# Gated linear attention scores computed on 64x64 diagonal squares, with the rotation split by token half, in a two-layer hybrid decoder trunk on one core

## The chip, the core and the metric

The kernel runs on one core of one Trainium2 chip. The metric is the device time of one execution in microseconds (us). The engines are PE (matrix multiply, with PEld for its weight loads), DVE (vector), ACT (scalar), POOL (GpSimd) and SP (which only issues transfers here). Each works through its own list of instructions in order; they meet at semaphores.

## What is computed

Two layers, 256 tokens, 1024 features. In each, one projection feeds three mixers (retention, RWKV-7, gated linear attention), whose outputs go through an output projection; then comes a retrieval over 16384 one-neuron experts. The change lies in the first two of these parts:

```python
z = h @ w_in[l]
z_ret, z_rwkv, z_gla = _split(z, GROUP_SIZES)
# retention: q and k are rotated, 4 heads of 64
q, k = _rotary(q, pos), _rotary(k, pos) * (RET_DK ** -0.5)
scores = jnp.einsum('bhid,bhjd->bhij', qc, kc) * dmat
# gated linear attention: 4 heads, keys of 48 (padded to 64 in the kernel), values of 96
bcum = jnp.cumsum(gc, axis=-2)
diff = bcum[..., :, None, :] - bcum[..., None, :, :]
dec = jnp.where(mask, jnp.exp(jnp.where(mask, diff, 0.0)), 0.0)
attn = jnp.sum(qc[..., :, None, :] * kc[..., None, :, :] * dec, axis=-1)
o = o_inter + jnp.einsum('bhij,bhjv->bhiv', attn, vc)
```

The kernel computes the gated scores of all 256 tokens as one lower triangle, by levels. Level 0 is the diagonal. Level n (1 to 8) holds the pairs whose tokens lie in the two halves of one block of 2^n tokens: both sides are scaled by the exponential of their distance to the block's middle, multiplied, and only the square of that level is kept.

## The kernel before, in words

The input projection is cut into 15 groups of 256 output columns. For a group, SP loads 1 MB of weights into one of two ring slots, ACT copies them in four parts to a rounded form (`w_high`, L1009), DVE forms the remainder of each part (`w_lows`, L1408), and PE multiplies with three products for each part (L417 to L419 for groups 0 to 7, L433 to L435 from group 8 on). The rounded form and the remainder have one buffer for each part: ACT may start part m of group g+1 when PE is done with part m of group g. ACT then moves the group's sum out of PSUM (`evac_group`, L1038 or L1040). Groups 10 to 13 are split by token half (`group(10, 0)`, `group(10, 1)`), each half with 24 matmuls of 128x256; a group in one piece has 48.

Between the half groups stand the levels. For level n, POOL forms the two differences (`level_gates(n)`, L1999 and L2000), ACT takes the exponential (L1220), POOL multiplies with queries and keys (`level_operand(n)`, L2008 and L2009), PE computes the scores (`level(n)`, L722), and DVE copies them under the level's mask into the sum `GACC` (L1656). For levels 0 to 7 PE runs, for each of two token tiles of 128 and four heads, one matmul with 64 rows (the key features), 128 columns of weights and 128 moving columns; heads with even and odd number use the two row halves of the array. PE's part of level n waits for `gx_ready` (POOL) and, where the scores go to the PSUM banks 4 and 5 or 6 and 7 in turn, for the readers of these banks. POOL's `level_operand(n)` waits until PE is done with level n-2, since its two buffers are used in turn.

Beside that, DVE rotates queries and keys of the retention (`rotate`, L1628 to L1633: six operations for each token tile), PE turns them (`turn_qk`, L682), ACT copies them out (L1228), PE multiplies them (`scores`, L690 and L691), DVE applies the decay (L1642 and L1643), and PE forms the outputs (`retention_outputs`, L702 to L705). All orders are written out by hand, one list for each engine, at the end of the engine's block. Behind group 14 follows the RWKV part (`units`, L517, L530 and L549), on 64x64 tiles of the array for part of its matmuls.

Of the kernel before, what the change touches and what calls it, by code (L numbers as in the profile page):

```python
# [33 lines left out]
U32 = mybir.dt.uint32  # L34
F16 = mybir.dt.float16
I32 = mybir.dt.int32
ALU = mybir.AluOpType
# [3 lines left out]
P = 128  # L41
S = 256
NT = S // P
# [57 lines left out]
def trunk(nc, x_in, w_in, w_out, cols, small, rows, norm_final, w_q, keys, u_t, v_t, const, xconst, out):  # L101
    with ExitStack() as ctx:
# [73 lines left out]
        LOWB, UPB, EYEB = LOWS[:, :, 0, :], LOWS[:, 0, 1, :], LOWS[:, 1, 1, :]  # L176
# [17 lines left out]
        GACC = BIG[:, decays:decays + 1536].rearrange("p (t h n) -> p t h n", t=3, h=GH)  # L194

# [67 lines left out]
        gacc_zero = sem("gacc_zero")  # L263
# [129 lines left out]
        def _(pe):  # L393
# [111 lines left out]
            def units():  # L505

                pe.wait_ge(ab_ready, 1)
                pe.wait_ge(gs_out, 9)

# [198 lines left out]
            def level(n, bank):  # L708
# [3 lines left out]
                for t in range(NT if n < 8 else 1):  # L712
                    for h in range(GH):
                        r, b = slice(64 * (h % 2), 64 * (h % 2) + 64), h // 2
                        if n == 0:
                            lhs, rhs = GQK[r, 2 + b, t * P:(t + 1) * P], GQK[r, b, t * P:(t + 1) * P]
                        elif n < 8:
                            lhs = rhs = GX[r, n % 2, b, t * P:(t + 1) * P]
                        else:
                            lhs, rhs = GX[r, n % 2, b, 0:P], GX[r, n % 2, b, P:S]  # L720
                        o = PS[:, bank + h % 2, (2 * t + b) * P:(2 * t + b + 1) * P]
                        mm = pe.matmul(o, lhs, rhs, start=True, stop=True)  # L722
                mm.then_inc(gs_done, 1)

            def gla_outputs():

                pe.wait_ge(proj_out, N_IN)
                for t in range(NT):
# [152 lines left out]
            with pe.Fori(0, L) as l:  # L881
# [23 lines left out]
                turn_qk()  # L905
                group(10, 1)
                pe.wait_ge(gs_out, 2)
                level(2, 4)
                pe.wait_ge(rot_out, 2)
                scores(0, 6)  # L910
                group(11, 0)
                pe.wait_ge(score_out, 2)
                level(3, 6)
                group(11, 1)
                pe.wait_ge(gs_out, 3)
                scores(1, 4)
                pe.wait_ge(gs_out, 4)
                level(4, 6)
                group(12, 0)
                pe.wait_ge(score_out, 4)  # L920
                level(5, 4)
                pe.wait_ge(gs_out, 5)
                retention_outputs()
                group(12, 1)
                pe.wait_ge(gs_out, 6)
                level(6, 4)
                group(13, 0)
                pe.wait_ge(ret_o_out, 1)
                level(7, 6)
                group(13, 1)  # L930
                pe.wait_ge(gs_out, 7)
                level(8, 4)
                group(14)
# [33 lines left out]
        def _(act):  # L967
# [52 lines left out]
            def w_split_in(g):  # L1020

                w_split(g)
# [128 lines left out]
            with act.Fori(0, L) as l:  # L1151
# [74 lines left out]
                for t in range(NT):  # L1226
                    act.wait_ge(rot_done, t + 1)
                    act.copy(QKT[:, :, t * P:(t + 1) * P], PS[:, 6 + t, :].rearrange("p (b n) -> p b n", b=4)).then_inc(rot_out, 1)  # L1228
                level_exp(3)
                w_split_in(11)  # L1230
                evac_group(10)
                level_exp(4)
                level_exp(5)
# [3 lines left out]
                act.copy(TI[:, :, :], EYEB.unsqueeze(1).broadcast_to([P, 12, 64])).then_inc(eye_ready, 1)  # L1237
                w_split_in(12)
                evac_group(11)
                level_exp(6)  # L1240
                act.copy(TB[:, :, :], EYEB.unsqueeze(1).broadcast_to([P, 12, 64])).then_inc(eye_ready, 1)
# [6 lines left out]
                level_exp(8)  # L1248
                w_split_in(14)
# [125 lines left out]
        def _(dve):  # L1375
# [244 lines left out]
            def rotate():  # L1620

                dve.wait_ge(proj_out, 10)
                for t in range(NT):
                    z = ZRET[:, t, 0:512].rearrange("p (g h c) -> p g h c", g=8, h=2)
                    rope = XC[:, X_ROPE + 64 * t:X_ROPE + 64 * (t + 1)].rearrange("p (a c) -> p a c", a=2)
                    cos, sin = (rope[:, a, :].unsqueeze(1).broadcast_to([P, 8, 32]) for a in range(2))
# [540 lines left out]
```

## Time and profile before

| | us |
|---|---|
| median of 3 runs (2082.27 to 2087.98) | 2083.05 |
| the profiled execution | 2079.46 |
| its span in the trace | 2077.7 |
| PE busy in the span | 2019.5 |
| stretch of the levels, layer 1 of 2 (81.60 to 131.70) | 50.10 |
| stretch of the levels, layer 2 of 2 (1111.90 to 1161.00) | 49.10 |

The profile shows one execution. A row of the timeline has its start in us from the span's start, its length in us, the engine, the line, the operation, what it writes and reads, the shape and the count; in brackets stands the idle time of the engine before it and who ended it. A matmul's modelled end reaches over the start of the next one, so that what a piece of work costs PE is read from start to start. An fp32 matmul appears as two records, so x16 is eight instructions. For the loop over the two layers the trace has the same lines twice.

### The profile page before, as it was taken

The page shows a single profiled execution, that of the slowest core. Times are in us where ns is not written, and L with a number is a line of the kernel's source. Part 1 is how long each engine was busy: PE and PEld are TensorE (multiplying, and loading weights), DVE is VectorE, ACT ScalarE, POOL GpSimd, SP SyncE. Part 2 cuts the span into 40 slices and gives each one's busy share as a digit, 9 for nine tenths or more (in the row PEclk, how much of TensorE's full clock was granted, in tenths as well). Part 3 has the DMA queues.
Part 4 walks back from the last instruction along what each step waited for, and adds up shares of the span by engine and source line. Part 5 has one row for each costly group of instructions (what it writes and reads, how often), then busy time and mean ns, then how long its engine had stood idle before and what let it go on. Part 6 is the DMA issues. An engine that isn't in the chain of part 4 may idle for free.

```text
span 2077.7 us, 47159 instructions
## 1 busy us (share of the span) xinstructions
PE 2019.5 (97%) x15444; PEld 1836.8 (88%) x15444; DVE 1416.5 (68%) x3068; ACT 1332.2 (64%) x3144; POOL 394.2 (19%) x348
## 2 busy tenths in 40 slices
PE   8999999999999999999999999999999999999996
PEld 8896899999999888888798959999999998888885
DVE  6863579588887666666668534985888876666665
ACT  6640555899999555555565315669999985555554
POOL 0312056522222000000004200764222220000000
PEclk9999999999999999999999999999999999999998
DMA  6311544444444555555553125444444445555554
GB/s 240 123 63 57 176 155 162 162 162 162 162 162 163 190 193 194 189 199 186 182 197 122 43 82 183 145 172 168 162 162 162 162 162 184 201 184 200 186 197 173
DMA packets 47471, 338.95 MB, mean 163 GB/s; under 512 B 5648, under 2 KB 5776, under 8 KB 6928
## 3 DMA queue, kind: packets, MB, share of 16 engines
q1 hardware_dynamic: 47376, 337.73, 45.5%
q8 instruction: 54, 0.88, 0.2%
q14 instruction: 41, 0.34, 0.0%
HBM read 336.66 MB, written 1.05 MB: 163 GB/s over the span
## 4 chain that ended last, share of the span: by engine, by line
PE 88%; DVE 7%; ACT 2%; DMA 1%; issue 1%; SPq 0%; DVEq 0%; ACTq 0%; PEldq 0%
PE ps L859 11%; PE ps L860 11%; PE ps L861 11%; PE ps L829 10%; PE ps L831 10%; PE ps L830 10%; PE ps L417 3%; PE ps L418 3%; PE ps L419 3%; PE ps L751 2%; PE ps L839 1%; PE ps L840 1%; PE ps L433 1%; DVE expert_lo L1786 1%; PE ps L435 1%; PE ps L434 1%
## 5 line engine op out<-in xcount | busy, mean ns | idle before, releaser
L829 PE MATMUL ps<-h_t_hi,expert_hi 128*128 128x256 f32 x2048 | 591.3, 289 | 12.3 <-DVE expert_lo L1786 8.6
L830 PE MATMUL ps<-h_t_lo,expert_hi 128*128 128x256 f32 x2048 | 578.5, 282 | 0.0
L831 PE MATMUL ps<-h_t_hi,expert_lo 128*128 128x256 f32 x2048 | 578.2, 282 | 0.0
L1980 POOL TENSOR_TENSOR expert_lo<-w_ring,expert_hi 128x512 fp32r<-128x512 f32 x204 | 289.7, 1428 | 719.2 <-ACT expert_hi L1050 717.6
L829 PEld LDWEIGHTS ps<-h_t_hi,expert_hi 128*128 128x128 f32 x2048 | 391.6, 191 | 15.6 <-ACT big L1055 8.3
L859 PE MATMUL ps<-expert_hi,act_hi 128*128 128x512 f32 x1008 | 392.1, 389 | 0.0
L860 PE MATMUL ps<-expert_lo,act_hi 128*128 128x512 f32 x1008 | 392.1, 389 | 0.0
L861 PE MATMUL ps<-expert_hi,act_lo 128*128 128x512 f32 x1008 | 392.1, 389 | 0.0
L830 PEld LDWEIGHTS ps<-h_t_lo,expert_hi 128*128 128x128 f32 x2048 | 391.9, 191 | 0.0
L831 PEld LDWEIGHTS ps<-h_t_hi,expert_lo 128*128 128x128 f32 x2048 | 391.6, 191 | 0.0
L1050 ACT CAST expert_hi<-w_ring 128x512 fp32r<-128x512 f32 x512 | 308.4, 614 | 98.2 <-PE ps L831 85.1
L1790 DVE TENSOR_TENSOR expert_lo<-w_ring,expert_hi 128x512 fp32r<-128x512 f32 x512 | 331.0, 687 | 6.7 <-ACT expert_hi L1130 6.0
L1140 ACT CAST act_hi<-big 128x256 fp32r (+1 forms) x256 | 103.9, 406 | 318.2 <-PE ps L861 318.2
L1130 ACT CAST expert_hi<-w_ring 128x512 fp32r<-128x512 f32 x512 | 291.9, 617 | 3.3 <-PE ps L831 3.2
L1786 DVE TENSOR_TENSOR expert_lo<-w_ring,expert_hi 128x512 fp32r<-128x512 f32 x308 | 217.7, 719 | 107.2 <-ACT expert_hi L1050 104.2
L1794 DVE TENSOR_TENSOR act_lo<-big,act_hi 128x256 fp32r<-128x256 f32 x256 | 108.8, 425 | 260.6 <-ACT act_hi L1140 260.6
L861 PEld LDWEIGHTS ps<-expert_hi,act_lo 128*128 128x128 f32 x1008 | 189.2, 188 | 39.4
L859 PEld LDWEIGHTS ps<-expert_hi,act_hi 128*128 128x128 f32 x1008 | 189.2, 188 | 39.2
L860 PEld LDWEIGHTS ps<-expert_lo,act_hi 128*128 128x128 f32 x1008 | 189.2, 188 | 39.1
L1408 DVE TENSOR_TENSOR expert_lo<-w_ring,expert_hi 128x512 fp32r<-128x512 f32 x188 | 131.7, 726 | 72.2 <-ACT expert_hi L1009 70.1
L1009 ACT CAST expert_hi<-w_ring 128x512 fp32r<-128x512 f32 x176 | 106.4, 619 | 107.8 <-PE ps L419 63.0
L417 PE MATMUL ps<-h_t_hi,expert_hi 128*128 128x256 f32 x512 | 146.4, 286 | 2.1 <-DVE expert_lo L1408 1.6
(310 smaller groups left out, 3133.8 us busy)
## 6 DMA issues: line engine op xcount, KB each, us to landing
w_ring<-u_t SPq DMA_DIRECT2D x128, 1024.0 KB, 4.8
w_ring<-v_t SPq DMA_DIRECT2D x128, 1024.0 KB, 4.8
w_ring<-w_in SPq DMA_DIRECT2D x32, 1024.0 KB, 4.9
w_ring<-w_q SPq DMA_DIRECT2D x16, 1024.0 KB, 4.8
w_ring<-w_out SPq DMA_DIRECT2D x8, 1024.0 KB, 4.8
big<-xconst SPq DMA_DIRECT2D x2, 1666.0 KB, 9.3
big<-keys SPq DMA_DIRECT2D x2, 1024.0 KB, 4.7
big<-rows SPq DMA_DIRECT2D x2, 576.0 KB, 11.2
```

The lines of the kernel that those rows point to most:

```text
L417: pe.matmul(o, w_hi_m[:, c, :], HTH[:, d, :], start=d == 0, stop=False)
L829: pe.matmul(o, w_hi[:, c, :], HTH[:, d, :], start=d == 0, stop=False)
L830: pe.matmul(o, w_hi[:, c, :], HTL[:, d, :], start=False, stop=False)
L831: mm = pe.matmul(o, w_lo[:, c, :], HTH[:, d, :], start=False, stop=d == DC - 1)
L859: pe.matmul(o, a_hi_t, EH[:, m % 4, :], start=start, stop=False, skip_group_check=True)
L860: pe.matmul(o, a_hi_t, EL[:, m % 4, :], start=False, stop=False, skip_group_check=True)
L861: mm = pe.matmul(o, a_lo_t, EH[:, m % 4, :], start=False, stop=True, skip_group_check=True)
L1050: act.copy(EH[:, m % 4, :], RING[:, m // 4, (m % 4) * 512:(m % 4 + 1) * 512]).then_inc(u_hi, 1)
L1130: act.copy(EH[:, m % 4, :], RING[:, m // 4, (m % 4) * 512:(m % 4 + 1) * 512]).then_inc(v_hi, 1)
L1786: dve.tensor_tensor(EL[:, m % 4, :], RING[:, m // 4, (m % 4) * 512:(m % 4 + 1) * 512], EH[:, m % 4, :].bitcast(F32), ALU.subtract).then_in ...
L1790: dve.tensor_tensor(EL[:, m % 4, :], RING[:, m // 4, (m % 4) * 512:(m % 4 + 1) * 512], EH[:, m % 4, :].bitcast(F32), ALU.subtract).then_in ...
L1980: pool.tensor_tensor(EL[:, m % 4, :], RING[:, m // 4, (m % 4) * 512:(m % 4 + 1) * 512], EH[:, m % 4, :].bitcast(F32), ALU.subtract).then_i ...
```

## The change

Levels 0 to 6 only ever need the two 64x64 squares on the diagonal of a 128-token tile. Now PE computes those alone: 16 matmuls with 64 rows, 64 columns of weights and 64 moving columns in the place of 8 with 128 and 128. Level 7 computes only the square of first-half keys and second-half queries. DVE copies levels 0 to 6 under folded masks (`UPF`, which POOL adds up from the left and right half of each mask) into a compact sum `GAC` of half the width, and level 7 straight into its place in `GACC`. ACT fills the zero square of `GACC` and copies the compact sum into its two diagonal squares behind level 6. Level 8 is as it was. All levels now use banks 4 and 5, and the retention banks 6 and 7. The orders on PE, ACT and DVE are written anew: the rotation is done by token half at two places, `turn_qk` comes behind group 11, which is in one piece, and group 14 is in two halves. The diff, cut to its core:

```diff
@@ -173,7 +173,9 @@
         LOWS = XC[:, X_LOW:X_LOW + 768].rearrange("p (n a b) -> p n a b", n=6, a=2)
-        LOWB, UPB, EYEB = LOWS[:, :, 0, :], LOWS[:, 0, 1, :], LOWS[:, 1, 1, :]
+        UPS = XC[:, X_UP:X_UP + 768].rearrange("p (n a b) -> p n a b", n=6, a=2)
+        LOWB, UPF, EYEB = LOWS[:, :, 0, :], UPS[:, :, 0, :], LOWS[:, 1, 1, :]
+        UPB = UPF[:, 0]
         VTOK = KKN.rearrange("p c n -> p (c n)").rearrange("p (k n) -> p k n", k=NT)
@@ -192,6 +194,8 @@
+
+        GAC = BIG[:, decays + 1728:decays + 2240].rearrange("p (t h n) -> p t h n", t=NT, h=GH)
@@ -506,6 +510,7 @@
                 pe.wait_ge(gs_out, 9)
+                pe.wait_ge(ret_o_out, 1)
 
@@ -712,19 +717,23 @@
-                        if n == 0:
-                            lhs, rhs = GQK[r, 2 + b, t * P:(t + 1) * P], GQK[r, b, t * P:(t + 1) * P]
-                        elif n < 8:
-                            lhs = rhs = GX[r, n % 2, b, t * P:(t + 1) * P]
+                        at = (2 * t + b) * 64
+                        if n < 7:
+                            for i in range(2):
+                                s = slice(t * P + 64 * i, t * P + 64 * i + 64)
+                                lhs, rhs = (GQK[r, 2 + b, s], GQK[r, b, s]) if n == 0 else (GX[r, n % 2, b, s], GX[r, n % 2, b, s])
+                                mm = pe.matmul(PS[64 * i:64 * i + 64, bank + h % 2, at:at + 64], lhs, rhs, start=True, stop=True)
+                        elif n == 7:
+                            mm = pe.matmul(PS[0:64, bank + h % 2, at:at + 64], GX[r, n % 2, b, t * P:t * P + 64], GX[r, n % 2, b, t * P + 64:(t + 1) * P],
+                                           start=True, stop=True)
...
-                            lhs, rhs = GX[r, n % 2, b, 0:P], GX[r, n % 2, b, P:S]
-                        o = PS[:, bank + h % 2, (2 * t + b) * P:(2 * t + b + 1) * P]
-                        mm = pe.matmul(o, lhs, rhs, start=True, stop=True)
+                            mm = pe.matmul(PS[:, bank + h % 2, b * P:(b + 1) * P], GX[r, n % 2, b, 0:P], GX[r, n % 2, b, P:S], start=True, stop=True)
...
+                pe.wait_ge(gacc_full, 3)
@@ -902,35 +911,35 @@
-                turn_qk()
...
+                group(11)
+                turn_qk()
+                pe.wait_ge(gs_out, 3)
+                level(3, 4)
...
-                group(11, 0)
+                group(12, 0)
+                pe.wait_ge(gs_out, 4)
+                level(4, 4)
...
-                level(3, 6)
-                group(11, 1)
-                pe.wait_ge(gs_out, 3)
-                scores(1, 4)
-                pe.wait_ge(gs_out, 4)
-                level(4, 6)
-                group(12, 0)
+                scores(1, 6)
+                group(12, 1)
+                pe.wait_ge(gs_out, 5)
+                level(5, 4)
...
-                level(5, 4)
-                pe.wait_ge(gs_out, 5)
...
-                group(12, 1)
+                group(13, 0)
...
-                group(13, 0)
-                pe.wait_ge(ret_o_out, 1)
-                level(7, 6)
...
+                level(7, 4)
+                group(14, 0)
+                pe.wait_ge(gs_out, 8)
...
-                group(14)
+                group(14, 1)
@@ -1223,22 +1232,23 @@
-                for t in range(NT):
-                    act.wait_ge(rot_done, t + 1)
-                    act.copy(QKT[:, :, t * P:(t + 1) * P], PS[:, 6 + t, :].rearrange("p (b n) -> p b n", b=4)).then_inc(rot_out, 1)
-                level_exp(3)
...
-                level_exp(4)
-                level_exp(5)
+                level_exp(3)
...
+                act.activation(GACC[64:128, 0:2, :, 0:64], EYEB[64:128].unsqueeze(1).unsqueeze(1).broadcast_to([64, NT, GH, 64]), ACT.Identity, scale=0.0).then_inc(gacc_full, 1)
...
+                for t in range(NT):
+                    act.wait_ge(rot_done, t + 1)
+                    act.copy(QKT[:, :, t * P:(t + 1) * P], PS[:, 6 + t, :].rearrange("p (b n) -> p b n", b=4)).then_inc(rot_out, 1)
...
+                level_exp(4)
+                level_exp(5)
+                act.copy(TB[:, :, :], EYEB.unsqueeze(1).broadcast_to([P, 12, 64])).then_inc(eye_ready, 1)
...
-                act.copy(TB[:, :, :], EYEB.unsqueeze(1).broadcast_to([P, 12, 64])).then_inc(eye_ready, 1)
@@ -1246,6 +1256,9 @@
+                act.wait_ge(gs_out, 7)
+                act.copy(GACC[0:64, 0:2, :, 0:64], GAC[0:64]).then_inc(gacc_full, 1)
+                act.copy(GACC[64:128, 0:2, :, 64:128], GAC[64:128]).then_inc(gacc_full, 1)
@@ -1617,21 +1630,20 @@
-            def rotate():
+            def rotate(t):

                 dve.wait_ge(proj_out, 10)
-                for t in range(NT):
-                    z = ZRET[:, t, 0:512].rearrange("p (g h c) -> p g h c", g=8, h=2)
...
+                z = ZRET[:, t, 0:512].rearrange("p (g h c) -> p g h c", g=8, h=2)
...
@@ -1643,7 +1655,8 @@
-            masks = [ident] + [XC[:, X_UP + P * n:X_UP + P * (n + 1)] for n in range(7)]
+            gac = GAC.rearrange("p t (c r) n -> p t r c n", r=2)
+            masks = [EYEB] + [UPF[:, n] for n in range(6)]
@@ -1651,9 +1664,11 @@
-                    if n < 8:
-                        mask = masks[n].bitcast(U32).unsqueeze(1).unsqueeze(1).broadcast_to([P, NT, 2, P])
-                        ins = dve.copy_predicated(gacc[:, 0:2, r], mask, PS[:, bank + r, :].rearrange("p (t c n) -> p t c n", t=NT, c=2))
+                    if n < 7:
+                        mask = masks[n].bitcast(U32).unsqueeze(1).unsqueeze(1).broadcast_to([P, NT, 2, 64])
+                        ins = dve.copy_predicated(gac[:, :, r], mask, PS[:, bank + r, 0:256].rearrange("p (t c n) -> p t c n", t=NT, c=2))
+                    elif n == 7:
+                        ins = dve.tensor_copy(gacc[0:64, 0:2, r, :, 64:128], PS[0:64, bank + r, 0:256].rearrange("p (t c n) -> p t c n", t=NT, c=2))
@@ -1889,22 +1904,24 @@
+                dve.wait_ge(folded, 1)
...
-                rotate()
+                rotate(0)
...
+                rotate(1)
...
+                w_lows(12)
+                level(3, 4)
...
-                level(3, 6)
-                w_lows(12)
-                decayed(1, 4)
-                level(4, 6)
+                level(4, 4)
+                decayed(1, 6)
+                w_lows(13)
...
-                w_lows(13)
...
-                level(7, 6)
...
+                level(7, 4)
@@ -2024,14 +2041,14 @@
-                pool.tensor_tensor(UPB, XC[:, X_UP:X_UP + 64], XC[:, X_UP + 64:X_UP + 128], ALU.add)
+                pool.tensor_tensor(UPF, UPF, UPS[:, :, 1, :], ALU.add)
...
-                pool.memset(GACC[:, 0:2, :, :], 0.0).then_inc(gacc_zero, 1)
+                pool.memset(GAC[:, :, :, :], 0.0).then_inc(gacc_zero, 1)
```

How the lists of two engines read around the rotation. On PE, from group 10 to the scores of the first two retention heads, before (L722 is a level, L433 to L435 a group, L682 `turn_qk`, L690 and L691 `scores`):

```order
L722 MATMUL ps<-big 128x128 [waits gx_ready,gs_out]
L722 MATMUL ps<-big 128x128 x7
L682 MATMUL ps<-const_sb,big 128x128 [waits rot_ready,gg_out]
L682 MATMUL ps<-const_sb,big 128x128 x3
L682 MATMUL ps<-const_sb,big 128x128 [waits rot_ready]
L682 MATMUL ps<-const_sb,big 128x128 x3
...
L722 MATMUL ps<-big 128x128 [waits gx_ready,gs_out]
L722 MATMUL ps<-big 128x128 x7
L690 MATMUL ps<-big 128x256 [waits rot_out]
```

And now (L725 is a level, L687 `turn_qk`, L695 `scores`; at the two marks stand the second half of group 10 and the whole of group 11):

```order
L725 MATMUL ps<-big 64x64 [waits gx_ready,gs_out]
L725 MATMUL ps<-big 64x64 x15
...
L725 MATMUL ps<-big 64x64 [waits gx_ready,gs_out]
L725 MATMUL ps<-big 64x64 x15
...
L687 MATMUL ps<-const_sb,big 128x128 [waits rot_ready,gg_out]
L687 MATMUL ps<-const_sb,big 128x128 x3
L687 MATMUL ps<-const_sb,big 128x128 [waits rot_ready]
L687 MATMUL ps<-const_sb,big 128x128 x3
L725 MATMUL ps<-big 64x64 [waits gx_ready,gs_out]
L725 MATMUL ps<-big 64x64 x15
L695 MATMUL ps<-big 128x256 [waits rot_out]
```

The transposes moved from between levels 1 and 2 to behind group 11, with level 3 between them and the scores. On DVE, from level 0 to level 2, now (L1669 is a level, L1640 to L1645 one token half of the rotation, L1421 the four remainders of a group; before, all twelve rows of the rotation stood between levels 0 and 1):

```order
L1669 COPY_PREDICATED big<-big,ps 128x4x64 [waits gs_done,gacc_zero,folded]
L1669 COPY_PREDICATED big<-big,ps 128x4x64
L1640 TENSOR_TENSOR big<-big 128x8x32 [waits proj_out]
...
L1669 COPY_PREDICATED big<-big,ps 128x4x64 [waits dve_step,gs_out,gs_done]
L1669 COPY_PREDICATED big<-big,ps 128x4x64
L1421 TENSOR_TENSOR expert_lo<-w_ring,expert_hi 128x512 [waits w_hi] x4
L1640 TENSOR_TENSOR big<-big 128x8x32 [waits proj_out]
...
L1669 COPY_PREDICATED big<-big,ps 128x4x64 [waits dve_step,gs_out,gs_done]
```

The second half of the rotation went behind level 1 and the remainders of group 11.

## Rows read from the trace of the kernel before

**Rows 1.** The page: busy times, chain by engine, transfers of the input weights.

```profile
PE 2019.5 (97%) x15444; PEld 1836.8 (88%) x15444; DVE 1416.5 (68%) x3068; ACT 1332.2 (64%) x3144; POOL 394.2 (19%) x348
...
PE 88%; DVE 7%; ACT 2%; DMA 1%; issue 1%; SPq 0%; DVEq 0%; ACTq 0%; PEldq 0%
...
w_ring<-w_in SPq DMA_DIRECT2D x32, 1024.0 KB, 4.9
```

**Rows 2.** Busy time by stretch: from:to, length, engines, granted clock, DMA.

```profile
81.60:131.70 50.10, 46.53 (x425) 43.93 (x424) 33.19 (x57) 20.73 (x36) 19.61 (x25) 0.97 0.31 109
...
91.55:96.08 4.53, 4.53 (x27) 4.40 (x25) 3.11 (x5) 2.86 (x5) 2.80 (x4) 0.62 0.00 2
...
140.00:150.00 10.00, 10.00 (x236) 9.48 (x234) 6.83 (x16) 7.32 (x37) 0.00 (x0) 1.00 0.01 2
...
1111.90:1161.00 49.10, 45.14 (x426) 42.43 (x424) 34.04 (x57) 20.78 (x36) 20.06 (x25) 1.00 0.31 111
```

**Rows 3.** Timeline of PE, first layer, levels 0 and 1 and the transposes.

```profile
81.62 1.16 PE L722 MATMUL ps<-big 64*128 64x128 f32 x16
82.71 0.39 PE L433 MATMUL ps<-expert_hi,h_t_hi 128*128 128x256 f32 x1
...
85.78 1.16 PE L722 MATMUL ps<-big 64*128 64x128 f32 x16
88.61 0.63 PE L682 MATMUL ps<-const_sb,big 128*128 128x128 f32 x4 [1.67 <-DVEq L1634]
91.14 0.66 PE L682 MATMUL ps<-const_sb,big 128*128 128x128 f32 x4 [1.90 <-DVEq L1634]
91.55 0.36 PE L433 MATMUL ps<-expert_hi,h_t_hi 128*128 128x256 f32 x1
```

**Rows 4.** Timeline of PE, second layer: the second transposes and level 3.

```profile
1121.47 0.66 PE L682 MATMUL ps<-const_sb,big 128*128 128x128 f32 x4 [1.90 <-DVEq L1634]
...
1130.28 1.16 PE L722 MATMUL ps<-big 64*128 64x128 f32 x16 [0.39 <-DVE big L1643]
```

**Rows 5.** Timeline of PE, first layer: matmuls of the RWKV part.

```profile
135.28 0.93 PE L530 MATMUL ps<-big 64*64 64x64 f32 x48
136.14 2.10 PE L517 MATMUL ps<-big 64*128 64x256 f32 x16
138.17 0.92 PE L549 MATMUL ps<-big 64*64 64x64 f32 x24
139.01 0.49 PE L517 MATMUL ps<-big 64*128 64x256 f32 x2
```

**Rows 6.** Timeline of DVE, both layers: levels, rotation, remainders of the weights.

```profile
83.65 1.39 DVE L1656 COPY_PREDICATED big<-const_sb,ps 128x512 f32<-128x512 uint32 x2
...
85.47 0.87 DVE L1629 TENSOR_TENSOR big<-big 128x256 f32<-128x256 f32 x1
...
88.89 0.42 DVE L1629 TENSOR_TENSOR big<-big 128x256 f32<-128x256 f32 x1
...
115.46 2.79 DVE L1408 TENSOR_TENSOR expert_lo<-w_ring,expert_hi 128x512 fp32r<-128x512 f32 x4 [2.95 <-ACT expert_hi L1009]
...
126.49 0.75 DVE L1658 COPY big<-ps 128x256 f32<-128x256 f32 x2
...
1123.82 4.10 DVE L1408 TENSOR_TENSOR expert_lo<-w_ring,expert_hi 128x512 fp32r<-128x512 f32 x4 [0.88 <-ACT expert_hi L1009]
```

**Rows 7.** Timeline of ACT, first layer: a copy out of PSUM and a fill.

```profile
89.27 0.59 ACT L1228 COPY big<-ps 128x512 f32<-128x512 f32 x1 [5.91 <-PE ps L682]
...
118.57 0.85 ACT L1245 ACTIVATE big<-big 64x768 f32<-64x768 f32 x1
```

**Rows 8.** Timeline of POOL, first layer: a mask's fold, a difference, a level's product.

```profile
18.35 1.10 POOL L2026 TENSOR_TENSOR big<-big 128x384 f32<-128x384 f32 x1 [11.36 <-DMA big<-rows]
...
85.45 0.61 POOL L1999 TENSOR_TENSOR big<-big 128x256 f32<-128x256 f32 x1 [0.18 <-POOL big L2009]
...
93.78 1.18 POOL L2009 TENSOR_TENSOR big<-big 128x256 f32<-128x256 f32 x1
```

More of the change, by code:

```diff
@@ L262, in trunk @@
         gla_o, gla_o_out = sem("gla_o"), sem("gla_o_out")
-        gacc_zero = sem("gacc_zero")
+        gacc_zero, gacc_full = sem("gacc_zero"), sem("gacc_full")
         silu_ready, gcum_ready, sq_ready = sem("silu_ready"), sem("gcum_ready"), sem("sq_ready")
@@ L1618, in rwkv_out @@
                 link(dve.tensor_tensor(O, O, GBIAS, ALU.add))
-            def rotate():
+            def rotate(t):
                 dve.wait_ge(proj_out, 10)
-                for t in range(NT):
-                    z = ZRET[:, t, 0:512].rearrange("p (g h c) -> p g h c", g=8, h=2)
-                    rope = XC[:, X_ROPE + 64 * t:X_ROPE + 64 * (t + 1)].rearrange("p (a c) -> p a c", a=2)
-                    cos, sin = (rope[:, a, :].unsqueeze(1).broadcast_to([P, 8, 32]) for a in range(2))
-                    tmp = RTMP[:, t, :].rearrange("p (g c) -> p g c", g=8)
-                    dve.tensor_tensor(ROT[:, t, :, 0, :], z[:, :, 0, :], cos, ALU.mult)
-                    link(dve.tensor_tensor(tmp, z[:, :, 1, :], sin, ALU.mult))
-                    link(dve.tensor_tensor(ROT[:, t, :, 0, :], ROT[:, t, :, 0, :], tmp, ALU.subtract))
-                    dve.tensor_tensor(ROT[:, t, :, 1, :], z[:, :, 0, :], sin, ALU.mult)
-                    link(dve.tensor_tensor(tmp, z[:, :, 1, :], cos, ALU.mult))
-                    link(dve.tensor_tensor(ROT[:, t, :, 1, :], ROT[:, t, :, 1, :], tmp, ALU.add))
-                    dve.sem_inc(rot_ready, 1)
+                z = ZRET[:, t, 0:512].rearrange("p (g h c) -> p g h c", g=8, h=2)
+                rope = XC[:, X_ROPE + 64 * t:X_ROPE + 64 * (t + 1)].rearrange("p (a c) -> p a c", a=2)
+                cos, sin = (rope[:, a, :].unsqueeze(1).broadcast_to([P, 8, 32]) for a in range(2))
+                tmp = RTMP[:, t, :].rearrange("p (g c) -> p g c", g=8)
+                dve.tensor_tensor(ROT[:, t, :, 0, :], z[:, :, 0, :], cos, ALU.mult)
+                link(dve.tensor_tensor(tmp, z[:, :, 1, :], sin, ALU.mult))
+                link(dve.tensor_tensor(ROT[:, t, :, 0, :], ROT[:, t, :, 0, :], tmp, ALU.subtract))
+                dve.tensor_tensor(ROT[:, t, :, 1, :], z[:, :, 0, :], sin, ALU.mult)
+                link(dve.tensor_tensor(tmp, z[:, :, 1, :], cos, ALU.mult))
+                link(dve.tensor_tensor(ROT[:, t, :, 1, :], ROT[:, t, :, 1, :], tmp, ALU.add))
+                dve.sem_inc(rot_ready, 1)
             def decayed(b, bank):
```

## The prediction

> **What bounds the kernel now.** I read the page first: PE is busy 97% of the span and holds 88% of the chain that ended last [rows 1]. So the question is only what the stretch of the levels costs PE. Then the busy time by stretch: of the 50.10 us in layer 1 PE is busy 46.53, in layer 2 45.14 of 49.10, and no other engine comes above 34.04 [rows 2]. The timeline of PE shows where the missing 3.6 and 4.0 us lie. Level 1 starts at 85.78 and costs 1.09 from start to start, as level 0 does (81.62 to 82.71); PE is then free at 86.87, but the first four transposes start at 88.61 and the second four at 91.14, both released by DVE's rotation; each four cost 0.41 (91.14 to 91.55) [rows 3]. The wait is 91.55 - 86.87 - 2 x 0.41 = 3.86 us. Layer 2 has the same wait, its second part again 1.90 us by the profile's count, and 0.39 us more before level 3, for DVE's decay, which reads the banks that level 3 writes [rows 4]. One thing more is seen in layer 1 alone: the half group behind the transposes takes 4.53 us at a granted clock of 0.62 [rows 2], where the half group at full clock takes 85.78 - 82.71 = 3.07 [rows 3]. Some of its matmuls ran at the lower level of 1.2 GHz, after PE had stood still twice.
>
> **The change part by part.**
>
> The levels on PE. The trace has the new shape already: L530 is a run of matmuls with 64 rows, 64 weight columns and 64 moving columns that goes through all four quarters of the array, two neighbours with the same rows and different output halves, as the new loop does. It takes 24 of them (48 records) from 135.28 to 136.14, 0.86 us, so 0.036 us each [rows 5]. Sixteen give 0.57 us for 1.09: 0.52 saved, seven times a layer. Level 7 has eight such matmuls into one output half, so two quarters take turns; the run that uses two quarters is L549, 12 in 0.84 us (138.17 to 139.01), 0.070 each [rows 5]. Eight give 0.56, 0.53 saved. A layer saves 7 x 0.52 + 0.53 = 4.17, both 8.3 us. The bounds are 0.57 and, at the rate of L549, 16 x 0.070 = 1.12 us for a level, which would save nothing. I take the first, since L530 has the same quarters in the same order. As the program is PE's nearly throughout, this falls on the path if nothing else is late.
>
> A rule of the Trainium skill speaks against this part: TensorE: Matmul & The Clock Gate, in Part 3, Packing small matmuls, says that a weight load overlaps running matmuls only where the row group differs, and the new inner loop keeps the row group. By that rule every second load would stand open and a level would gain little or nothing. This case's trace doesn't agree: in L530 every second matmul keeps its rows too, and it is the cheapest run of the three [rows 5].
>
> The rotation. It is 3.6 us of DVE for the first token half (from 85.04, where level 0's copy ends, to the release at 88.61) and 2.53 for the second (88.61 to 91.14) [rows 3, 6]. Now PE has other work while it goes on. I follow both lists from 81.62, with DVE done with the remainders of group 10 at 83.65. DVE: level 0 to 84.35, first half to 87.95, level 1 to 88.65, remainders of group 11 (2.79, [rows 6]) to 91.45, second half to 94.0 (95.05 if it takes 3.6), level 2 to 94.7 (95.75). PE: level 0 to 82.19, half group to 85.26, level 1 to 85.83, half group to 88.90, then level 2, which needs DVE's level 1: 0.25 us to spare. Level 2 to 89.47; the first remainder of group 11 is there at 89.35, and the next come every 0.70 where PE takes 0.74 for a quarter. Group 11, 24 matmuls twice, takes 2 x 3.07 less a little, to 95.5; the transposes find the second half done. So the wait of 3.86 goes in both layers: 7.7 us. With it goes the low clock, 4.53 - 3.07 = 1.46 us, since PE doesn't stand still there, and the 0.39 us of layer 2, since levels and retention have banks of their own.
>
> What is late next. Between transposes and scores stands level 3, 0.57 us. ACT does its last quarter of group 12's weights when PE is done with group 11, then two copies of 0.59 us [rows 7]; the second can't start before the last transpose. That makes about 1 us from there to the release of the scores, 0.4 more than level 3 covers: 0.8 us lost in both layers.
>
> The levels on DVE. A copy of 128x512 under a mask is 1.39 us for two [rows 6]. For 128x256 I have the plain copies out of PSUM, 0.75 for two; the bounds are half of 1.39 and the whole. I take 0.70. It counts through the schedule above alone. At 1.39 level 1 would end 1.4 later, and level 2 on PE would wait 1.2 us.
>
> ACT. New are a fill of 64x512 and two copies of 64x512. The nearest rows are 0.59 (128x512 copy) and 0.85 (64x768 fill) [rows 7]; I take 0.6 each. The fill lies in time in which ACT waits for group 11. The two copies wait for DVE's level 6, and behind them on ACT stands group 14's weight split, for which DVE and then PE wait. From PE's level 6 on: 0.57, DVE 0.70, copies 1.2, the first quarter of the split 0.6 like the copy of the same size, DVE 0.70, together 3.8; PE has level 6, a half group and level 7 meanwhile, 0.57 + 3.07 + 0.56 = 4.2. It is hidden with 0.4 to spare; at 0.85 a copy it would cost 0.1 us a layer. The compact sum's last copies are done 15 us before the matmuls that read them.
>
> POOL. Its fold grows to 128x384, at most 1.10 us like its neighbour, at 18 us of the layer, long before its use at 83; the fill of zeros halves. The levels' operands are as before: differences and products of 0.61 to 1.18 us each [rows 8], some 3.5 to 4.5 for a level. The slots on PE are 3.64 us now for 4.16, but around them stand group 11, scores and outputs. The narrowest is level 4: ACT takes its exponential behind the transposes' copies, two products follow, and level 4 is due 3.07 us plus the scores after that. Hidden. SP has no transfer more; the loads of 4.9 us [rows 1] have two half groups and two levels, 7.3 us, each.
>
> The sum: 8.3 + 7.7 + 1.5 + 0.4 - 0.8 = 17.1 us. From the profiled execution, 2079.46, that gives 2062.4; from the median of the three runs, 2083.05, 3.6 us above it, 2066.0. I predict for the median.
>
> **The rivals.**
>
> DVE becomes the bound around the rotation. Its work from level 0 to the remainders of group 12 is 13.5 to 16 us in a stretch that PE now crosses in 15, with 0.1 to 0.3 us to spare at the first steps. For it speaks that beside POOL the same rotation operation takes 0.87 for 0.42, and four remainders 4.10 for 2.79 [rows 6]. If both sets of remainders take 4.10, group 11's last quarter comes 1 us late and the next steps again some 0.5 to 1. Two layers give 3 to 5 us, so 2070. Against it: POOL is quiet between its products of level 2 and 3, where group 11's remainders fall. The Trainium skill, GPSIMD Engine Reference, 1. Specifications, gives the reason: POOL's SBUF interfaces are shared with VectorE and contend with instructions that have two SBUF inputs. The trace agrees, with 0.87 against 0.42.
>
> The small matmuls don't pack. A level stays at 1.12 us, the 8.3 us are gone, and the waits alone are saved: 8.8, so 2074.3. Only L549 speaks for it.
>
> The clock falls: slower than before. The stretch puts more small matmuls between the groups, and if PE's clock goes to 1.2 GHz there and stays, a group's matmuls cost more. The low stretch lost 0.38 x 4.53 = 1.7 us of clock and cost 1.46 us, 0.85 for each. At half clock throughout, the 30.5 us of groups in a layer would take 30.5 / (1 - 0.85 x 0.5) = 53, 22.6 us more, both layers 45, so 2111. It decides from 17.1 / 45 = 38% of the groups' work at the low level. For it speaks only the one low stretch, which came after standing still; against it, that the RWKV part, with 236 matmul records of mostly 64x64 in 10 us, kept 1.00 [rows 2].
>
> The change doesn't do what it says: the second half of the rotation is late for the transposes by as much as before. It would have to end 4 us later than I have it. I give it next to nothing.
>
> **How the numbers follow.** My forecast 0.72, DVE the bound 0.17, no packing 0.06, the clock 0.03, and 0.02 for a fall of waits that I don't see. The likeliest gives 2066.0. Below it lie the 0.8 us of new waits and low clock that may go elsewhere, some 2 us, and the runs' own spread, of which the three of before show 0.8 us below the median and 4.9 above. Above it lie 2070 to 2071 of the DVE case and 2074.3. So 2061 to 2075. What a measurement of this kernel can tell from no change is about 0.3%, 6.2 us, so faster means below 2076.8: 0.92. Within it fall half of the packing case with an added wait, and the unseen: 0.05. Slower 0.03.
>
> **What would show it.** A level on PE of 0.57 us from start to start (rival: 1.1); no idle time before the transposes; level 2 and group 11 without a wait for DVE (rival: PE waits for L1421 or L1669 there, 1 us and more); 0.4 us idle before the scores, ended by ACT; a granted clock of 1.00 throughout the stretch; the stretches some 41 us long in both layers. I am wrong if PE waits for DVE, ACT or POOL more than 2 us a layer in the stretch, or if the stretches shrink and the time comes back in the RWKV part behind them.

## The result, and the profile after

| | before | after |
|---|---|---|
| first runs, median (us) | 2085.35 (4 runs) | 2064.29 (2063.83 to 2065.5, 4 runs) |
| ratio, 95% interval | | 0.9905 (0.9886 to 0.9924) |
| a second series (run e3_after) | 2081.32 (2079.76 to 2092.1, 23 runs) | 2064.61 (2063.87 to 2074.88, 6 runs), ratio 0.9921 (0.9899 to 0.9944) |
| span of the profiled execution | 2077.7 | 2062.0 |
| stretch of the levels, layer 1 | 50.10 | 41.84 |
| stretch of the levels, layer 2 | 49.05 | 41.86 |

The kernel became faster by 15.7 us from trace to trace, of which 8.26 and 7.19 lie in the two stretches, and by 17 to 21 us from median to median. I had forecast 17.1 and 2066.0. Two executions, one of 9508 us of the kernel before and one of 2837 us of e8_later, lie far above all others of their kernels and are left out of the ratios below.

Busy time by stretch, after (from:to, length, engines, granted clock):

```profile
81.75:123.59 41.84, 41.63 (x537) 39.17 (x536) 30.03 (x57) 22.30 (x39) 19.64 (x25) 1.00 0.36 130
1103.78:1145.64 41.86, 41.62 (x537) 39.19 (x536) 30.02 (x57) 22.31 (x39) 19.66 (x25) 1.00 0.36 130
81.75:96.00 14.25, 14.15 (x195) 13.60 (x195) 13.60 (x24) 8.37 (x16) 7.19 (x9) 1.00 0.45 158
```

PE is busy for all but 0.2 us of a stretch, where it missed 3.6 and 4.0 [rows 2], and the clock is 1.00 in both. In the first 14.25 us DVE is busy 13.60: it is nearly full where the rotation lies. The timeline of PE, after, answers to [rows 3]:

```profile
81.75 0.69 PE L725 MATMUL ps<-big 64*64 64x64 f32 x32
82.37 0.39 PE L437 MATMUL ps<-expert_hi,h_t_hi 128*128 128x256 f32 x1
...
88.92 0.28 PE L439 MATMUL ps<-expert_hi,h_t_lo 128*128 128x256 f32 x1
89.30 0.69 PE L725 MATMUL ps<-big 64*64 64x64 f32 x32
89.97 0.36 PE L437 MATMUL ps<-expert_hi,h_t_hi 128*128 128x256 f32 x1
...
95.79 1.04 PE L687 MATMUL ps<-const_sb,big 128*128 128x128 f32 x8
96.83 0.69 PE L725 MATMUL ps<-big 64*64 64x64 f32 x32
97.63 0.71 PE L695 MATMUL ps<-big 64*128 64x256 f32 x4
...
115.97 0.28 PE L439 MATMUL ps<-expert_hi,h_t_lo 128*128 128x256 f32 x1
116.18 0.68 PE L727 MATMUL ps<-big 64*64 64x64 f32 x16
116.84 0.36 PE L437 MATMUL ps<-expert_hi,h_t_hi 128*128 128x256 f32 x1
```

A level takes 0.62 us from start to start (81.75 to 82.37), where it took 1.09. No idle time stands before the transposes. Small waits are left, each seen as a start that comes late: level 2 starts 0.10 after the modelled end of the half group before it (88.92 + 0.28), where level 7 starts 0.07 before it (116.18 for 115.97 + 0.28), so level 2 waits 0.17; the eight transposes take 1.04 where two fours took 0.41 each, so 0.22 is a wait; the scores start 0.80 after level 3, which costs 0.62, so they wait 0.18. Together that is 0.57 us a layer. The scores start when ACT has copied the turned queries and keys (timeline of ACT, after):

```profile
96.52 1.07 ACT L1246 COPY big<-ps 128x512 f32<-128x512 f32 x2
```

The timeline of DVE, after, answers to [rows 6]:

```profile
84.44 0.41 DVE L1640 TENSOR_TENSOR big<-big 128x256 f32<-128x256 f32 x1
...
87.82 0.43 DVE L1645 TENSOR_TENSOR big<-big 128x256 f32<-128x256 f32 x1
88.47 0.78 DVE L1669 COPY_PREDICATED big<-big,ps 128x256 f32<-128x256 uint32 x2 [0.22 <-DVE big L1645]
89.15 2.49 DVE L1421 TENSOR_TENSOR expert_lo<-w_ring,expert_hi 128x512 fp32r<-128x512 f32 x4
91.55 0.96 DVE L1640 TENSOR_TENSOR big<-big 128x256 f32<-128x256 f32 x1
...
95.35 0.43 DVE L1645 TENSOR_TENSOR big<-big 128x256 f32<-128x256 f32 x1
96.00 0.78 DVE L1669 COPY_PREDICATED big<-big,ps 128x256 f32<-128x256 uint32 x2 [0.22 <-DVE big L1645]
```

The two copies of a level take 0.68 us (88.47 to 89.15), near the 0.70 that I took. The second half of the rotation goes from 91.55 to 95.78, 4.2 us, where I had 2.5 to 3.6. It ends as PE gets to the transposes. POOL works beside most of it, on its two products for level 3 and the two differences for level 5 (timeline of POOL, after):

```profile
91.02 1.21 POOL L2025 TENSOR_TENSOR big<-big 128x256 f32<-128x256 f32 x1 [3.85 <-ACT big L1229]
92.19 0.92 POOL L2026 TENSOR_TENSOR big<-big 128x256 f32<-128x256 f32 x1
93.29 0.61 POOL L2016 TENSOR_TENSOR big<-big 128x256 f32<-128x256 f32 x1 [0.18 <-POOL big L2026]
93.86 0.84 POOL L2017 TENSOR_TENSOR big<-big 128x256 f32<-128x256 f32 x1
```

### The profile page after: what moved, and what is told of

Same layout as the page of the kernel before. It is cut to its first block, busy times and chain, and to the rows that moved or that the text cites. A ratio compares the mean times of both kernels' runs of the same rounds, so it can differ in the third digit from the quotient of the medians.

```text
span 2062.0 us, 47617 instructions
## 1 busy us (share of the span) xinstructions
PE 2012.1 (98%) x15668; PEld 1829.9 (89%) x15668; DVE 1412.5 (69%) x3068; ACT 1335.4 (65%) x3150; POOL 394.8 (19%) x348
## 4 chain that ended last, share of the span: by engine, by line
PE 87%; DVE 8%; ACT 3%; DMA 1%; issue 1%; SPq 0%; DVEq 0%; ACTq 0%; PEldq 0%
PE ps L868 11%; PE ps L869 11%; PE ps L870 11%; PE ps L838 10%; PE ps L840 10%; PE ps L839 10%; PE ps L421 3%; PE ps L422 3%; PE ps L423 3%; PE ps L760 2%; PE ps L848 1%; PE ps L849 1%; PE ps L437 1%; DVE expert_lo L1801 1%; PE ps L439 1%
## 5 line engine op out<-in xcount | busy, mean ns | idle before, releaser
L838 PEld LDWEIGHTS ps<-h_t_hi,expert_hi 128*128 128x128 f32 x2048 | 391.6, 191 | 15.7 <-ACT big L1064 8.3
L1421 DVE TENSOR_TENSOR expert_lo<-w_ring,expert_hi 128x512 fp32r<-128x512 f32 x188 | 131.0, 730 | 64.8 <-ACT expert_hi L1018 62.5
```

Source lines behind the costliest of these rows:

```text
L838: pe.matmul(o, w_hi[:, c, :], HTH[:, d, :], start=d == 0, stop=False)
```

## The experiments

All are compared with the kernel before on the same chip. The stretch is from the start of level 0 to the start of the RWKV part's first matmul, layer 1 and layer 2.

| run | what | span | stretches | ratio (95%) |
|---|---|---|---|---|
| e1_order | new orders, old levels | 2068.8 | 45.21, 45.22 | 0.9951 (0.9934 to 0.9967) |
| e2_squares | new levels, old orders | 2073.5 | 47.06, 48.50 | 0.9968 (0.9957 to 0.9979) |
| e3_after | the changed kernel | 2062.1 | 41.86, 41.85 | 0.9921 (0.9899 to 0.9944) |
| e4_control | the kernel before | 2078.9 | 51.07, 50.11 | 1.0005 (0.9992 to 1.0019) |
| e5_halves | squares in another order | 2065.2 | 43.35, 43.36 | 0.9922 (0.9903 to 0.9942) |
| e6_rot_both | rotation in one piece | 2070.8 | 46.02, 46.36 | 0.9958 (0.9943 to 0.9972) |
| e7_wide | wide copies on DVE | 2065.1 | 43.31, 43.34 | 0.9922 (0.9903 to 0.9941) |
| e8_later | scores later | 2062.1 | 41.63, 41.62 | 0.9909 (0.9883 to 0.9934) |
| e9_rows | squares in a third order | 2062.2 | 41.85, 41.84 | 0.9913 (0.9893 to 0.9933) |
| e10_moves | e8 and two moves more | 2063.0 | 41.50, 41.47 | 0.9928 (0.9900 to 0.9955) |

The runs of the kernel before spread from 2079.4 to 2092; of the ten of the changed kernel nine lie within 2063.8 to 2065.6 and one took 2074.88. So the ratios alone don't part kernels that lie 2 to 3 us from each other. For those the stretches in the traces decide: the stretch of the changed kernel came out between 41.84 and 41.86 us in two traces, both layers.

**e1_order and e2_squares: the two parts alone.**

```diff
 # e1_order: orders as changed; level() on PE and DVE, GACC and masks as before
-                            mm = pe.matmul(PS[64 * i:64 * i + 64, bank + h % 2, at:at + 64], lhs, rhs, start=True, stop=True)
+                        mm = pe.matmul(PS[:, bank + h % 2, (2 * t + b) * P:(2 * t + b + 1) * P], lhs, rhs, start=True, stop=True)
 # e2_squares: level(), GAC, UPF as changed; the three lists between level 0 and units() as before
-                rotate(0)
-                level(1, 4)
-                w_lows(11)
-                rotate(1)
-                level(2, 4)
+                rotate(0)
+                rotate(1)
+                level(1, 4)
+                w_lows(11)
+                level(2, 4)
```

> The new orders on PE, ACT and DVE, with levels of 64x128 matmuls, wide masked copies and no compact sum, as before. Theory (two separate gains: shorter levels, and the waits of the rotation): the two waits of 3.86 us go, level costs stay 1.09 us, so a stretch of the levels of 41.85 + 7 x 0.47 + 0.44, less the 0.28 us wait before the scores that a longer level 3 covers, about 45.3 us, in both layers, and a span near 2069. Rival (the new orders only pay with the short levels and narrow copies, since DVE is full around the rotation): PE waits for DVE 1 us or more before level 2 or in group 11, stretch above 46.5, span above 2071.

> The 64x64 squares and the compact sum alone, with the orders of before (rotation in one piece before level 1, transposes between levels 1 and 2). Theory of two separate gains: levels 0.62 us on PE, stretches 3.7 us shorter than 50.1 and 49.1 less what the wait for the rotation grows (PE comes 0.9 us earlier, DVE 0.6), so 46.7 and 45.7, span 2071 to 2072. Rival (the wait takes back what the levels before it give, and later levels wait for POOL): stretches shorter by 2 us or less. In both the PE waits before the transposes stay at 1.7 to 2.2 us each, and the granted clock may fall behind them.

The orders alone came out as the theory had them: 45.21 us for 45.3, span 2068.8 for 2069. The squares alone gave less, 2073.5 for 2071 to 2072. Their stretch is near the theory in layer 1 (47.06 us for 46.7) and far from it in layer 2 (48.50 for 45.7). The timeline of PE in e2_squares, layer 1 and layer 2, and then layer 2 by stretch, say why:

```profile
87.93 0.63 PE L686 MATMUL ps<-const_sb,big 128*128 128x128 f32 x4 [2.33 <-DVEq L1645]
90.46 1.11 PE L686 MATMUL ps<-const_sb,big 128*128 128x128 f32 x4 [1.90 <-DVEq L1645]
95.14 0.69 PE L724 MATMUL ps<-big 64*64 64x64 f32 x32
...
1117.91 1.11 PE L686 MATMUL ps<-const_sb,big 128*128 128x128 f32 x4 [1.90 <-DVEq L1645]
1124.08 0.69 PE L724 MATMUL ps<-big 64*64 64x64 f32 x32
```

```profile
1108.71:1157.21 48.50, 44.31 (x537) 41.78 (x537) 29.26 (x57) 22.59 (x39) 18.67 (x25) 0.93 0.32 112
...
1118.00:1124.00 6.00, 6.00 (x28) 5.85 (x28) 3.48 (x5) 2.97 (x5) 3.32 (x4) 0.50 0.00 0
```

The wait before the transposes is 2.33 us for 1.67 [rows 3]: of the 0.94 us that two short levels save ahead of it, it takes back 0.66. And behind the pauses the clock fell, in layer 2 also, to 0.50 for the 6 us shown. What a fall costs is seen from the start of the second transposes to the start of level 2, which is 0.41 + 3.07 = 3.48 us at full clock [rows 3]: 4.68 us in layer 1 of e2_squares and 6.17 in layer 2, so 1.2 and 2.7 us are lost; in the trace of before the first layer lost 1.46 and the second nothing.

The parts alone save 8.9 and 4.2 us of span, 13.1, together 15.7. The missing 2.6 are no single effect. The low clock makes 2.4: e2_squares lost 3.9 us by it and before 1.5. The longer wait makes 1.3 in both layers. About 1 us goes the other way, half of it outside the stretches; it isn't accounted for here. Without the falls the squares alone are worth about 6.0 us in the two stretches, and 6.7 on top of the new orders (45.21 - 41.84 and 45.22 - 41.86).

**e3_after and e4_control: the same kernels again.** No edit.

> The changed kernel once more, beside the same runs of the kernel before as the others. Theory: span 2062 again and stretches of 41.8 us, 15.7 us less than the profiled execution of before. The timed difference was 19.8 us (15.8 to 23.8), 4 more; theory for these: the runs of before spread (2079.5 to 2088) with low stretches of the clock behind PE's pauses, so the timed difference stays above 15.7. Rival: chance of few runs, the difference comes out at 16 us or less.

> The kernel before, unchanged, against itself: how far two series of the same kernel come apart, and whether the low clock behind the transposes of layer 1 (0.62 over 4.5 us) comes again. Theory (clock falls are free of place, they follow pauses of PE): ratio 1.000 within 0.002, the low stretch at another place or missing, span within 2076 to 2084 according to it. Rival (the low stretch belongs to this place): the same 4.5 us at 0.62 in layer 1 and none in layer 2.

The stretches of the changed kernel are the same to 0.02 us. The control is at 1.0005, and its profiled execution at 2078.9 for 2077.7 has low stretches of the clock in both layers, where before had one:

```profile
91.05:96.19 5.14, 5.14 (x27) 5.00 (x25) 3.20 (x5) 2.97 (x5) 3.31 (x4) 0.54 0.00 2
1120.00:1125.00 5.00, 3.17 (x20) 3.17 (x21) 3.80 (x8) 2.74 (x5) 1.21 (x2) 0.82 0.00 0
```

The half group behind the transposes takes 5.14 us here, 4.53 in [rows 2], 3.07 at full clock [rows 3]. So neither expectation holds whole: a fall belongs to the place (behind the two pauses), but its length differs from run to run, and in layer 2 it comes in some executions. The spread of the kernel before has one source there; that it is the only one isn't shown, and the stretches of the control are 2.0 us longer than those of before while its span is 1.2 longer. Whether the timed difference is really above the 15.7 us of the traces is open: the first series gives 16 to 24 by its interval and the second 12 to 21.

**e5_halves and e9_rows: the order of the squares in a level.**

```diff
 # e5_halves
-                for t in range(NT):
-                    for h in range(GH):
-                        for i in range(2):
+                for i in range(2):
+                    for t in range(NT):
+                        for h in range(GH):
 # e9_rows: p is h % 2, b is h // 2
+                for t in range(NT):
+                    for b in range(2):
+                        for i in range(2):
+                            for p in range(2):
```

> The changed kernel with the loop over the two 64-token squares outermost in levels 0 to 6: the same 16 matmuls, first the eight into the upper output half, then the eight into the lower, so two neighbours differ in rows but not in output half. Theory (a level is cheap because its neighbours go through all four quarters of the array): back to two quarters at a time, 16 x 0.070 = 1.1 us a level instead of 0.62, stretches of 45.3 us, span 2069. Rival (the size alone makes them cheap, whatever the order): level 0.62, span 2062.

> The changed kernel with levels 0 to 6 in the order token tile, head pair, square, head of the pair: every matmul changes the rows against the one before it, the output half changes every second time; in the changed kernel it is the other way round. Theory (all four quarters in turn make a level cheap, in whatever order): 0.62 us a level as now. Rival (a weight load hides only behind a matmul with other rows): now every second load stands open, so the new order is faster, 0.5 us or less a level, stretches of 41.0, span 2060.5.

Timeline of PE, level 0 and what follows it, e5_halves and then e9_rows:

```profile
81.65 0.98 PE L724 MATMUL ps<-big 64*64 64x64 f32 x32
82.55 0.39 PE L437 MATMUL ps<-expert_hi,h_t_hi 128*128 128x256 f32 x1
```

```profile
81.35 0.69 PE L724 MATMUL ps<-big 64*64 64x64 f32 x32
81.98 0.39 PE L437 MATMUL ps<-expert_hi,h_t_hi 128*128 128x256 f32 x1
```

With two quarters at a time a level takes 0.90 us, not the 1.1 of my expectation, but 0.28 more than with four. Which of rows or output half changes at every step makes no difference: 0.63 for 0.62. So the theory holds in kind (four quarters in turn) and is too large in size, and the rival of the open weight loads falls: with rows changing at every step nothing is gained in e9_rows, and e5_halves, whose rows change at every step too, is the slowest of the three orders. About 0.28 of the 0.47 us that a level saves hang on the four quarters in turn; the other 0.19 stay with two at a time. What the 0.90 is made of stays open. Seven levels of 0.28 are 2.0 us a layer, and the stretch grew by 1.5 only: with longer levels the small waits before level 2 and before the scores are gone, and PE is busy 43.35 of 43.35 us.

**e6_rot_both: the rotation in one piece, the transposes behind group 11.**

```diff
                 rotate(0)
+                rotate(1)
                 level(1, 4)
                 w_lows(11)
-                rotate(1)
                 level(2, 4)
```

> The changed kernel with both token halves of the rotation before level 1 on DVE; PE's and ACT's orders as changed. Theory (the split by token half is needed, because DVE has no time to spare before level 2): DVE ends level 1 2.5 to 4 us later, PE waits that long before level 2, stretches longer by 2.5 to 4 us each; the clock may fall behind so long a pause for 1 to 1.5 us more; span 2067 to 2072. Rival (moving the transposes behind group 11 was enough, the split is idle): span within 1.5 us of 2062.

PE and then DVE in the timeline, and the stretch from level 2 to the transposes:

```profile
91.83 1.10 PE L725 MATMUL ps<-big 64*64 64x64 f32 x32 [2.73 <-DVE big L1669]
```

```profile
88.31 0.43 DVE L1640 TENSOR_TENSOR big<-big 128x256 f32<-128x256 f32 x1
...
90.36 0.42 DVE L1645 TENSOR_TENSOR big<-big 128x256 f32<-128x256 f32 x1
91.00 0.78 DVE L1669 COPY_PREDICATED big<-big,ps 128x256 f32<-128x256 uint32 x2 [0.22 <-DVE big L1645]
```

```profile
91.83:99.87 8.04, 7.94 (x80) 7.78 (x81) 5.67 (x8) 2.08 (x4) 2.40 (x3) 0.79 0.37 133
```

The theory holds: PE stands still 2.73 us before level 2, then runs at a mean clock of 0.79 through level 2 and group 11 (8.04 us, where the changed kernel takes 95.79 - 89.30 = 6.49, so 1.55 of the longer stretch is low clock). The stretches are 4.2 and 4.5 us longer and the span 8.8 us. Without the split more than half of the gain would be gone, though the transposes stand where the change put them. The DVE rows show the second half in a time in which POOL runs nothing (it is idle from 87.08 to 90.92): 88.31 to 90.79, 2.5 us for the 4.2 in the changed kernel.

**e7_wide: narrow squares, wide copies.**

```diff
 # on DVE; PE writes each square to its place on the diagonal of a 128-wide area, and ACT's fill and two copies are gone
-                        ins = dve.copy_predicated(gac[:, :, r], mask, PS[:, bank + r, 0:256].rearrange("p (t c n) -> p t c n", t=NT, c=2))
+                        ins = dve.copy_predicated(gacc[:, 0:2, r], mask, PS[:, bank + r, :].rearrange("p (t c n) -> p t c n", t=NT, c=2))
```

> The changed kernel with 64x64 squares on PE but copies of 128x512 under unfolded masks on DVE straight into the full sum, no compact sum and no copies on ACT. Theory (DVE is full around the rotation, so the width of its copies counts there and only there): 0.6 us more a copy; level 2 waits 1.2 us more, and some of the later steps up to the scores as well; stretches 1.2 to 2.5 us longer, span 2064.5 to 2067. Rival (copies are hidden behind the half groups everywhere): span within 0.5 us of 2062.

Timeline of PE, level 2 and group 11:

```profile
89.93 0.69 PE L725 MATMUL ps<-big 64*64 64x64 f32 x32 [0.95 <-DVE big L1664]
...
93.39 0.39 PE L437 MATMUL ps<-expert_hi,h_t_hi 128*128 128x256 f32 x1 [0.16 <-DVE expert_lo L1416]
```

0.95 us idle before level 2 and 0.16 in group 11, for the remainders that come late. The stretch is 1.5 us longer, the span 3.0. DVE's copies, which by DVE's share in the profile of before (68% [rows 1]) would be taken for hidden, are on the path at two places once PE is fast; the compact sum with its folded masks, not only the short matmuls, is needed for the 15.7: without it 12.6 are left.

**e8_later and e10_moves: the waits that are left.**

```diff
 # e8_later, on PE; the second scores and the retention outputs move by a half group in the same way,
 # and DVE's decay of the second scores goes behind the remainders of group 13
-                scores(0, 6)
                 group(12, 0)
+                pe.wait_ge(rot_out, 2)
+                scores(0, 6)
 # e10_moves, besides; first on PE, then on DVE
-                turn_qk()
                 level(3, 4)
+                turn_qk()
...
-                rotate(1)
                 level(2, 4)
+                rotate(1)
```

> The changed kernel with the first scores behind the first half of group 12 instead of before it, the second scores and the retention outputs one half group later too, and DVE's decay of the second scores behind the remainders of group 13. Theory (PE waits 0.28 us for ACT's copies before the scores in each layer): this goes, span 0.5 us shorter, 2061.5, which only the profile can tell. Rival (another wait takes its place, for the decay or before level 8): span 2062 or longer.

> The order of the run with the later scores, and beside it level 3 before the transposes on PE, and level 2 before the second half of the rotation on DVE. Theory (DVE has nothing to spare before the transposes: the second four wait 0.22 us for the rotation): this goes too, a stretch 0.2 us shorter than with the later scores alone, 41.4 us, span 2061 to 2062. Rival (the wait moves on to group 12, whose remainders now come behind the rotation): stretch 41.6 or longer, with PE idle in front of group 12 or in its first quarter, ended by DVE.

By stretch, e8_later:

```profile
81.53:123.16 41.63, 41.52 (x538) 39.22 (x537) 29.86 (x57) 22.31 (x39) 19.67 (x25) 1.00 0.36 131
```

And e10_moves, with a place in layer 2's expert search:

```profile
81.56:123.06 41.50, 41.40 (x537) 39.20 (x536) 29.08 (x57) 22.41 (x39) 19.60 (x25) 1.00 0.37 131
1370.00:1375.00 5.00, 4.13 (x23) 4.14 (x24) 5.00 (x14) 0.69 (x2) 1.88 (x2) 0.70 0.60 210
```

Each move takes from the stretch, 0.21 us where 0.28 was expected and then 0.13 where 0.2 was, but the spans are 2062.1 and 2063.0 for 2062.0, not the 2061.5 and 2061 to 2062 expected: what lies outside the stretch varies by more. In e10_moves the clock fell once at 1370 us, far from the edit. Neither beats the changed kernel by anything that can be measured, and no faster version was found.

## Why the prediction was right, step by step

- What bounds the kernel, and the waits of 3.86 us a layer: right. The waits are gone in the trace after, and e1_order, where nearly only they go, has the stretch expected for it.
- The levels: mechanism right, size a little off. I read 0.57 us from L530 at 0.036 us a matmul [rows 5]; it is 0.62, and level 7 is 0.66 (116.18 to 116.84) for 0.56. 0.05 for fourteen levels and 0.1 for two make 0.9 us of the 1.4 by which the forecast of 17.1 was above the 15.7 of the traces. A rate from a run of 24 matmuls was used for runs of 16 and 8; a fixed cost per run may be behind it, but was not measured by itself. Another 0.3 us are new waits: 1.1 in both layers where 0.8 were counted (next point).
- What is late next: right about ACT. Its second copy ends at 97.59, 1.0 us after the 0.82 that eight transposes need, as worked out, and the scores start at 97.63. But the 0.4 us of waiting that I had put before the scores are split: the transposes wait 0.22 for the rotation and the scores 0.18 for ACT. New is the 0.17 before level 2, where I had 0.25 to spare. The term that was mis-sized is the rotation on DVE. I gave the second half 2.5 to 3.6 us and it takes 4.2; the first takes 3.8, and 4.0 up to level 1's copy, for 3.6. Beside the second stand POOL's products for level 3 and the differences for level 5 (91.02 to 94.70); the same six operations take 2.5 where POOL runs nothing (e6_rot_both). I had noted that POOL is quiet between its products of levels 2 and 3, which held for the remainders (2.49 for four), and not asked what POOL does behind that. That it is POOL that makes them longer is read from the rows (those that lie beside a POOL operation are long, those behind the last one aren't); no run changes POOL alone.
- The DVE rival (0.17) was wrong in its price, 3 to 5 us, but right about the place: DVE has no slack there. e6_rot_both and e7_wide show that 2.5 us more a layer on DVE ahead of level 2 cost 8.8 of the span (low clock included), and copies 0.6 us longer each cost 3.0.
- The no-packing rival was wrong (0.62 for 1.12). The rule of the Trainium skill (TensorE: Matmul & The Clock Gate, Part 3, Packing small matmuls) that a weight load overlaps only where the row group differs made no difference to a level here, so the trace doesn't agree: e9_rows, in which it always differs, has 0.63 us a level for 0.62, and e5_halves, in which it always differs too, 0.90.
- The clock: right in direction. It stays at 1.00 in both stretches. The 1.46 us that I counted for layer 1 is one draw of something that varies: 4.53, 5.14 and 3.07 us were seen for the same half group, and e2_squares lost 2.7 us in one layer.
- DVE's narrow copy (0.68 for 0.70), ACT's fill and copies (0.63, 0.62 and 0.61 for 0.6) and the hidden wait for level 6: as forecast. Group 14 starts without a wait.
- From the profiled execution I predicted 2062.4; the first execution after took 2063.8. That the median of before lies 3.6 us and more above its profiled execution, and that of after 0.5, is why the timed gain is larger than the worked one. I had carried the 3.6 over unchanged, which made the forecast 3.1 us too late, while the terms made it 1.4 too early; the two errors partly cancel, and that 2066.0 lies only 1.7 us from 2064.29 is in part luck.

## What to carry to other kernels

Where a wait stands behind some work on the waiting engine, shortening that work gives its time to the wait; take the wait away first, and the same shortening counts nearly in full. Here two of the seven short levels stood ahead of it, and 0.66 of their 0.94 us were lost. Before such parts are added up, read from each trace what the clock took: here its falls differed by 2.4 us between the two traces, as much as the parts alone seemed to miss. Once PE is dense, follow the engine that feeds it instruction by instruction over the stretch: what its total share calls idle may be full for the 14 us that matter, and the order of its work is then worth more than its length. Price an operation on DVE that may meet POOL by what POOL runs at that time in the new order, not by the row of the old one.

## What the hardware showed that I had not expected

- DVE's six rotation operations of 128x256 took 2.5 us with POOL quiet and 4.2 us with POOL's products and differences beside most of them, a factor of 1.7: 0.41 to 0.43 us each alone, 0.76 to 1.07 beside POOL in the trace after.
- Sixteen 64x64 matmuls took 0.62 us over four quarters of the array in both orders tried and 0.90 us over two quarters at a time. The 0.070 us a matmul of L549, which also uses two quarters [rows 5], does not carry over to them.
- After two pauses of PE of 1.7 to 2.3 and 1.9 us with one run of four transposes between them, the granted clock fell to the lower level for some us in layer 1 of all three traces of these orders and in layer 2 of two of them (before, e4_control, e2_squares); after one pause of 2.7 us it fell also (e6_rot_both, both layers). In these traces the gain from a removed pause is larger than the pause, by 0 to 2.7 us.
